# A routing product in four column tiles, experts chosen from unscaled products, and rows normalised behind the choice

## The reference

```python
x = x + jnp.einsum('bse,ed->bsd', mix, w_out)
x = x + _hier_moe(_rmsnorm(x, g_ffn), ...)
# _hier_moe, h = normalised rows
pg = softmax(h @ w_rg)                    # 4 groups
g_sel = argmax(pg); p_sel = pg[g_sel]
le_sel = (h @ w_re)[experts of g_sel]     # 8 of 32
pe = softmax(le_sel)
top_p, top_i = top_k(pe, 2); top_p = top_p / sum(top_p)
gate = p_sel * top_p
# each token through its two experts: (silu(x @ w_g) * (x @ w_u)) @ w_d, times gate, added
```

## Time and profile before

| | us |
|---|---|
| median of 3 runs (1562.38 to 1566.72) | 1566.23 |
| profiled execution | 1563.33 |
| its span, first to last instruction | 1561.8 |
| TensorE busy | 1438.2 (92%) |
| VectorE busy | 1091.8 (70%) |
| ScalarE busy | 871.1 (56%) |
| GpSimd busy | 283.3 (18%) |

### The profile page before, as it was taken

One profiled execution on the slowest core, in us unless ns is written; L12 is line 12 of the kernel. 1 busy time (PEld: TensorE's weight loads), 2 busy tenths in 40 slices (PEclk: granted clock), 3 DMA queues, 4 the chain that ended last, 5 costly groups with the idle time before them and its releaser, 6 DMA issues.

```text
span 1561.8 us, 22918 instructions
## 1 busy us (share of the span) xinstructions
PE 1438.2 (92%) x8088; PEld 1193.5 (76%) x8088; DVE 1091.8 (70%) x1645; ACT 871.1 (56%) x1148; POOL 283.3 (18%) x270
## 2 busy tenths in 40 slices
PE   6999999999988899986999959999999999999993
PEld 4888788888876678775888847787787877878771
DVE  5666766343456676673466669888888888888886
ACT  6434444334445554453434437777777777777764
POOL 0000111111133000000122131511121221222431
PEclk9999999999999999998999969999999999999996
DMA  7232322222121110013466338999999999999997
GB/s 242 88 100 95 129 89 70 89 81 75 48 88 48 53 30 14 28 48 113 137 216 241 108 149 309 381 373 381 379 383 384 382 375 379 383 380 375 384 345 296
DMA packets 77483, 322.84 MB, mean 207 GB/s; under 512 B 13542, under 2 KB 22118, under 8 KB 52834
## 3 DMA queue, kind: packets, MB, share of 16 engines
q1 hardware_dynamic: 60722, 273.77, 46.8%
q0 software_dynamic: 16688, 48.10, 10.1%
HBM read 278.77 MB, written 51.80 MB: 212 GB/s over the span
## 4 chain that ended last, share of the span: by engine, by line
DMA 22%; PE 12%; DVE 11%; issue 6%; ACT 2%; DVEq 0%; ACTq 0%; SPq 0%; POOLq 0%; POOL 0%
DMA plain<-in_w_down 20%; DVE split L1812 8%; PE acc L96 3%; PE acc L97 3%; PE acc L98 3%; PE acc L2008 1%; ACT split L2519 1%; PE acc L1999 1%; DMA s_x_mid<-plain 1%; ACT shared L1806 1%; DVE plain L2630 0%; DMA plain<-s_h_rows,plain 0%; DVE x_late L2630 0%; DVE shared L1812 0%; DMA plain<-s_x_mid 0%
## 5 line engine op out<-in xcount | busy, mean ns | idle before, releaser
L1806 ACT CAST shared<-plain 128x2048 fp32r<-128x2048 f32 x190 | 361.9, 1915 | 111.5 <-DMA plain<-in_w_up 76.9
L96 PE MATMUL acc<-shared,split 128*128 128x512 f32 x952 | 381.5, 401 | 15.1 <-DVE split L2065 10.3
L98 PE MATMUL acc<-shared,split 128*128 128x512 f32 x952 | 373.0, 392 | 0.0
L1812 DVE TENSOR_TENSOR split<-plain,shared 128x2048 fp32r<-128x2048 f32 x126 | 282.6, 2283 | 0.6 <-ACT shared L1806 0.6
L96 PEld LDWEIGHTS acc<-shared,split 128*128 128x128 f32 x952 | 180.3, 189 | 52.6 <-DVE split L2065 10.5
L98 PEld LDWEIGHTS acc<-shared,split 128*128 128x128 f32 x952 | 179.7, 189 | 38.7
L96 PE MATMUL pa<-shared,a_xT_hi 128*128 128x512 f32 (+1 forms) x480 | 194.0, 404 | 4.2 <-DVE a_w_lo L747 3.3
L97 PE MATMUL acc<-split 128*128 128x512 f32 x504 | 196.5, 390 | 0.0
L98 PE MATMUL pa<-shared,a_xT_lo 128*128 128x512 f32 (+1 forms) x480 | 187.1, 390 | 0.0
L97 PE MATMUL acc<-shared,split 128*128 128x512 f32 x448 | 176.2, 393 | 0.0
L1812 DVE TENSOR_TENSOR shared<-plain,shared 128x2048 fp32r<-128x2048 f32 x64 | 145.9, 2281 | 3.2 <-ACT shared L1806 3.2
(11 more groups left out here) (322 smaller groups left out, 2521.0 us busy)
## 6 DMA issues: line engine op xcount, KB each, us to landing
plain<-in_w_gate SPq DMA_DIRECT2D x64, 1024.0 KB, 9.8
plain<-in_w_up SPq DMA_DIRECT2D x64, 1024.0 KB, 11.6
plain<-in_w_down SPq DMA_DIRECT2D x64, 1024.0 KB, 10.8
a_x_sb<-in_x SPq DMA_DIRECT2D x24, 512.0 KB, 4.1
s_mid<-a_kv SPq DMA_DIRECT2D x12, 512.0 KB, 2.9
a_kv<-s_mid SPq DMA_DIRECT2D x12, 512.0 KB, 3.6
plain<-s_mixT SPq DMA_DIRECT2D x12, 512.0 KB, 7.0
plain<-in_x SPq DMA_DIRECT2D x12, 512.0 KB, 3.9
```

What stands on the lines that cost most here:

```text
L96: pe.matmul(out, st_hi, mv_hi, start=first, stop=False)
L98: return pe.matmul(out, st_lo, mv_hi, start=False, stop=last)
L1806: eng.copy(self.w_hi[j // 2][:, cols], self.source(j)).then_inc(self.s_whi[j], 1)
L1812: eng.tensor_tensor(self.w_lo[j // 2][:, cols], self.source(j), self.w_hi[j // 2][:, cols].bitcast(F32), ALU.subtract).then_inc(self.s_wlo ...
```

## The change

Three things are done in `phase_mix`:

1. The routing product of a tile is made in four column tiles. Each of the 8 calls with 128 columns of weights becomes four with 32 columns, which write 32 partitions of the result each: 32 calls in place of 8.
2. The choice of group and experts reads the unscaled products. A row's scale is positive and so changes no order. The exponential of the odds takes it as its scale instead and waits for the reciprocal.
3. The reciprocal and the normalised rows are made behind the choice, not ahead of the split and the choice.

```diff
                 for k in range(KD):
-                    ins = pe.matmul(pr[:, 0:NG + NE], hT[:, k * P:(k + 1) * P], w_r[:, k, :],
-                                    start=k == 0, stop=k == KD - 1)
+                    for q in range(4):
+                        some = slice(q * P // 4, (q + 1) * P // 4)
+                        ins = pe.matmul(pr[some, 0:NG + NE], hT[:, k * P + some.start:k * P + some.stop], w_r[:, k, :],
+                                        start=k == 0, stop=k == KD - 1, tile_position=(0, some.start))
                 ins.then_inc(s_r, 1)
...
                 act.wait_ge(s_odds, t + 1)
-                nc.scalar.activation(part[:], odds[:], ACT.Exp).then_inc(s_part, 1)
+                act.wait_ge(s_rstd, t + 1)
+                nc.scalar.activation(part[:], odds[:], ACT.Exp, scale=rstd[:, 0:1]).then_inc(s_part, 1)
...
-                dve.wait_ge(s_root, t + 1)
-                nc.vector.reciprocal(rstd[:], root[:]).then_inc(s_rstd, 1)
-                dve.wait_ge(s_rstd, t + 1)
-                nc.vector.scalar_tensor_tensor(out=h_sb[:, half, :], in0=x2[:, half, :], scalar=rstd[:, 0:1],
-                                               in1=g_row[:], op0=ALU.mult, op1=ALU.mult).then_inc(s_h, 1)
                 if not (isinstance(r, int) and r == TILES // 2 - 1):
                     split(t + 2, half)
                 dve.wait_ge(s_r, t + 1)
-                steps.chain(nc.vector.tensor_scalar(g8[:, 0:NG], pr[:, 0:NG], rstd[:, 0:1], None, ALU.mult))
+                steps.chain(nc.vector.tensor_copy(g8[:, 0:NG], pr[:, 0:NG]))
...
-                nc.vector.scalar_tensor_tensor(out=lem[:], in0=pr[:, NG:NG + NE], scalar=rstd[:, 0:1], in1=mask[:],
-                                               op0=ALU.mult, op1=ALU.mult).then_inc(s_rev, 1)
+                nc.vector.tensor_tensor(lem[:], pr[:, NG:NG + NE], mask[:], ALU.mult).then_inc(s_rev, 1)
...
                 steps.end()
+                dve.wait_ge(s_root, t + 1)
+                nc.vector.reciprocal(rstd[:], root[:]).then_inc(s_rstd, 1)
+                dve.wait_ge(s_rstd, t + 1)
+                nc.vector.scalar_tensor_tensor(out=h_sb[:, half, :], in0=x2[:, half, :], scalar=rstd[:, 0:1],
+                                               in1=g_row[:], op0=ALU.mult, op1=ALU.mult).then_inc(s_h, 1)
```

## The result

| | before | after |
|---|---|---|
| median of 7 runs each (range), us | 1564.89 (1562.38 to 1566.72) | 1557.0 (1553.9 to 1560.37) |
| profiled execution, us | 1563.33 | 1556.43 |
| its span, us | 1561.83 | 1554.92 |

The ratio is 0.9949, with a 95% interval of 0.9934 to 0.9963: the changed kernel is faster by half a per cent. A second set of six runs, in the last group of experiments, gave 1556.21 us and 0.9947 (0.9927 to 0.9967).

A forecast was written before the change was run, and what follows sets the result against it. TensorE was taken to bound tiles 0 to 10, a chain of waits up to the gather the end. Terms -3.5 + 4.6 = +1.1 us took 1563.33 to 1564.4, shifted by 2.9 to 1567.3 us; range 1558.5 to 1577.5.

The forecast's parts named there:

- Products 0 to 9: Routing products under a full TensorE: 17.5 ns a pair in four column tiles, saving 0.32 us a tile, 3.5 in eleven.
- issue floor: Rival, routing product: a pair takes 29 ns whatever its tile, so slower, 1576.9 us; chance 0.18.
- the rival without any overlap: Routing product: load and matmul of 27 and 30 ns in a row, 3.6 us a product, 1597 us; chance 0.04.
- Switching in and out: TensorE around each product: 0.32 us into narrow tiles, then 0.15 and 0.34 us out of them.
- Rows behind the choice in the tiles: Tiles 0 to 9: the moved 1.46 us on VectorE is covered by idle time, with 0.8 us of cover; cost 0.
- The end: Tiles 10 and 11: the gather waits for the landing of the last normalised rows, 919.23 to 923.8 us, +4.6 us.
- all four tiles at once: Rival, routing product: four column tiles overlap fully, 0.5 us in place of 1.12, 1559.3 us; chance 0.15.
- Delay taken up: Rival, behind the gather: another wait ends last, so only the product's saving is left, 1562.7 us; chance 0.10.

The follow-up runs named there:

- halves: The changed kernel with the routing product in two column tiles of 64 columns in place of four of 32; 1561.92 us in one run.
- alone-run: The kernel before with the unscaled choice and the normalised rows behind it, the product left whole; 1568.0 us (10 runs), ratio 1.0033.
- rows ahead: The changed kernel with reciprocal and normalised rows of every tile back ahead of the choice; 1554.54 us (4 runs), once more 1553.37 us (5 runs).
- four alone: The kernel before with only the routing product split into four column tiles; 1552.93 us (5 runs), once more 1556.35 us (6 runs).
- the rows made elsewhere: The changed kernel with tile 10's rows ahead of its choice and tile 11's made by GpSimd and ScalarE; 1553.26 us (6 runs), ratio 0.9933.

## Why the prediction was wrong

**Products 0 to 9: right in kind, wrong in size, and this is the step that failed.** They gave 9.33 us where I had 3.2. The prediction said "only the second pass of one tile and the first of the next overlap. So a pair is half of 53.5 ns plus some 2.5", which gave 17.5 ns. It is 9.1: 0.57 us for the body in place of 1.12. The runs show another rule. A column tile works through its own pairs one after another, one every 33 ns with 32 columns and every 58 with 64, and as many tiles run side by side as the order of the calls keeps supplied:

| order | tiles at work | pairs | starts within, us | from a pair to the next of its tile, ns |
|---|---|---|---|---|
| k outside, four tiles | 4 | 64 | 0.571 | 33 |
| two calls of a tile as neighbours | 4, less near the changes | 64 | 0.670 | |
| two tiles at a time | 2 | 64 | 0.941 | 33 |
| tile by tile | 1 | 64 | 1.761 | 33 |
| halves | 2 | 32 | 0.902 | 58 |
| undivided | 1 | 16 | 1.589 | 112 |

(The last column is read from the single starts of the product of tile 2, behind the first of them: the length of one round, a start in each tile at work. That it is a tile's own step is the reading that makes all orders agree; the trace doesn't name the tile of a start. In the fourth line each of the three changes of tile saves some 0.1 us, when pairs of the next tile start beside the last ones of the tile before: 63 x 33 ns less three times 0.105 us is 1.76.)

The inference came from the earlier trace rows: two loads of four had started by 221.54 us, and I read "they come in twos" as a limit on what overlaps. Those loads have 64 columns (the 128*64 of their line), and with 64 columns there are only two column tiles. Twos were all that could be seen, and the row could not tell "two at once" from "all tiles at once". The same holds for the 29 ns of the earlier trace rows: 58 ns in each of two tiles, neither a floor in the issue nor a limit of pairs. Halves gave 29.1 again. The issue floor, to which I gave 0.18, and the rival without any overlap are refuted by the 9.1 ns.

The Trainium skill's "TensorEngine Tiling (Array Packing)", Instruction Overhead, gives a matmul some 60 cycles. Within one tile no run here contradicts that, since a pair every 33 ns is 79 cycles at 2.4 GHz. What the trace contradicts is the sum over all 64 matmuls that the prediction made of it: over four tiles a pair starts every 9.1 ns, 22 cycles for a load and a matmul together. The Trainium skill's "TensorE: Matmul & The Clock Gate", Part 3, has column tiles start some 4 ns apart and run together, and with the running together the trace agrees: four pairs start within 20 ns, 6 to 7 ns apart.

**Switching in and out: right.** 0.32 us into the narrow tiles (782.78 to 783.10), then 783.80 to 784.13, 0.33, back; I had 0.32 and 0.34. From the last narrow start to the wide one are 0.13 us, for which I had 0.15.

**Rows behind the choice in the tiles: right.** Cost 0, by the alone-run's 142.82 us and by rows ahead's 133.49, both equal to their partners. The copies on ScalarE lost some margin, not TensorE's time: 1.54 us are left of 1.91, where I had counted on 0.8.

**The end: right in its parts, and the sum smaller because of the product again.** From the choice of tile 10 to its sum +1.21 us (890.89 to 896.03 against 900.20 to 904.13), forecast +1.36. Last product to its choice 1.25 us in place of 3.2, where I had 2.6: at the lower clock (0.50 in this stretch against 0.58 before) the pairs take 0.93 us and not the 2.24 of 17.5 doubled. Last choice -0.5 us, forecast -0.6; the pause of the earlier trace rows at 911.28 went, since GpSimd issues nothing beside it now. In all five executions where GpSimd issues the rows' transfer at this place, VectorE pauses for 0.54 us between the same two steps of the choice, and in the nine others for 0.15. From the end of the last choice to the gather I had 8.5 (915.3 to 923.8) and it is 8.65 (904.69 to 913.34): rows 1.39, to the issue 0.6, landing 5.16, to the gather 1.5. For the moved rows without the quicker last product my sum is 4.6 + 0.6 = +5.2 us to the gather; the alone-run has +5.7. The 0.5 between them is its last product, which ran at the lower clock all through (granted clock 0.50 against 0.58 before) and started its pairs within 3.22 us, not 2.77. In the whole change product 10 (-0.9) and product 11 (-1.96) take most of the +5.2 off again, which leaves the +2.3 measured from product 10 to the gather.

**Not foreseen: 0.8 us back behind the gather.** The turns follow 6.95 us after the gather instead of 7.75, in the alone-run 6.68. In both, GpSimd's issue of the gather is 1.06 us long in place of 2.69, since VectorE's wide split beside it began earlier and met the table write instead (last section). It goes the same way in all fourteen executions: the turns follow after 6.7 to 7.2 us where that issue is short (1.05 to 1.08 us), and after 7.7 to 8.5 where it is long (2.68 to 3.18). That is a coincidence of lines; it was not tested by itself.

**The sum of it.** On the profiled executions I forecast +1.1 us and measured -6.9. Of these 8.0 us, 6.1 are the ten products and 2.0 the end up to the gather (+2.3 where I had +4.3); the 0.8 behind the gather and 0.2 behind the turns were not foreseen, and a first phase that was 1.1 us longer hid as much again, by chance. Another 2.3 us come from the 2.9 that I added between profiled execution and median: it was 0.6 in the kernel after.

**The rival that came true** was "all four tiles at once", at a chance of 0.15 and 1559.3 us. On the profiled execution it had said 1563.33 + 1.1 - 6.8 - 1.2 = 1556.4 us; the profiled execution after took 1556.43. Up to the gather that agreement is the mechanism's, -6.9 by its sum and -7.0 measured. To the hundredth it is luck: the +1.13 of the first phase happened to cancel the -0.80 and -0.21 behind the gather. The 2.9 us between profiled execution and median were of three runs; seven put before's median at 1564.89, 1.6 above the profiled one, so that the same sum gives 1558.0, 1.0 above the measured median. "Delay taken up" was wrong: what the gather loses or gains passes through, since the stretch from the turns to the end stayed between 633.1 and 635.7 us in every kernel.

The price of my choice between 17.5 and 8 ns was 0.55 us a product, and the profile had no tile of 32 columns to choose by. The middle would not have been right either; what should have been seen is that the evidence was from a case with two tiles only.

## What to carry over

This fp32 product with few moved columns was bound by its weight loads, and splitting the columns of its weights over four column tiles cut it from 1.6 to 0.57 us, but only with the tiles taking turns: the same calls tile by tile took 1.76 us. Before taking a row of a trace as a limit, ask whether the limit could have shown in it at all; loads of 64 columns can't show more than two at once. Work that is moved behind the critical choice of a loop can be free in the loop and still has to be moved back in its last rounds, where a transfer and a gather wait for it: here 3.15 of the 11 us that the rest had won up to the turns were given back there, and the version with the rows ahead keeps them (1553.5 us against 1556.7 in the medians of all runs).

## What the runs showed of the hardware

- Column tiles are independent: pairs of load and matmul start every 9.1 ns over four tiles, 14.9 over two, 33 within one (32 columns of weights, 36 moved, fp32). Two neighbouring calls on one tile hold the others up by 0.10 us a product, eight by all that there is to win. How far TensorE looks past waiting pairs was not measured.
- GpSimd and VectorE are slow beside each other. The first indirect issue of GpSimd that begins beside VectorE's first wide splits (L1812, 4.48 us for two) takes 2.7 to 3.2 us and not 1.0, in all fourteen executions: the gather's before (2.69), with four alone and with rows ahead (2.68 to 2.69) and the rows made elsewhere (3.18), the second table write's in the kernel after (3.00) and in all the others (3.00 to 3.02). In the other direction, a VectorE comparison of 0.35 us took 2.15 beside GpSimd's multiplication of 128x1024 and ended 0.09 us after it. What they share was not tested, nor whether ScalarE's work or the transfers of the same time have a part in the first. The kernel after, GpSimd and then VectorE:

```profile
908.89 3.00 POOL L1938 DMA_INDIRECT s_table<-plain  x1 [0.30 <-issue]
913.34 1.06 POOL L2318 DMA_INDIRECT plain<-s_h_rows,plain  x1 [1.46 <-issue]
```

```profile
908.73 4.48 DVE L1812 TENSOR_TENSOR shared<-plain,shared 128x2048 fp32r<-128x2048 f32 x2
```

- The last of the twelve transfers of normalised rows landed 4.9 to 5.5 us after its issue in all fourteen executions, however the stage's end was arranged (median of the twelve 3.0 before). It was the slowest in all but one: with halves the first took 6.1 us. Why it is slow is open.
- With the last product the granted clock is 0.50, the lower of the two levels, and its 64 pairs start within 0.93 us, 1.6 times the 0.57 at full clock; a round of four takes 60 ns in place of 33. The undivided one took 3.22 against 1.59 where it ran at 0.50 all through (rows behind the choice alone), and 2.77 before, at 0.58.
